# Two attentions of a fused two-block kernel: where the softmax division is done

## The reference, cut to what matters

```python
def gqa_block(q_blk, k, v):                      # first block
    s = jnp.einsum('bkgqd,bksd->bkgqs', q_blk, k).astype(jnp.float32) * (HEAD_DIM ** -0.5)
    p = jax.nn.softmax(s, axis=-1)
    return jnp.einsum('bkgqs,bksd->bkgqd', p.astype(v.dtype), v)
...
    a_out = attention_branch(q, k, v, q_g, k_g, cos, sin, n_tok) * jax.nn.silu(a_gate)
...
def block(args):                                 # second block, MLA
    s = jnp.einsum('bhqd,bhkd->bhqk', qi, kt).astype(jnp.float32) * scale
    s = jnp.where(mask[None, None], s, -1e30)
    pr = jax.nn.softmax(s, axis=-1).astype(vt.dtype)
    return jnp.einsum('bhqk,bhkd->bhqd', pr, vt)
```

## Time and profile before

| what | us |
|---|---|
| median of 3 runs | 2500.69 |
| the profiled execution, its own time | 2496.18 |
| its span (first to last instruction) | 2494.4 |
| first attention | about 360 to 626 |
| MLA | about 1146 to 1460 |
| mean granted TensorE clock | 0.919 of full speed |

### The profile page before, as it was taken

The page is one execution under the profiler, slowest core; times in us unless marked ns, Lnnn a source line. Parts: engine busy times, 40 slices in busy tenths (PEclk is TensorE's granted clock), DMA queues, the critical chain, the costliest instruction groups (busy, mean ns, idle before and its releaser), DMA issues.

```text
span 2494.4 us, 24100 instructions
## 1 busy us (share of the span) xinstructions
PE 2153.5 (86%) x9931; PEld 1760.8 (71%) x9931; DVE 1213.3 (49%) x1423; ACT 606.8 (24%) x1035; POOL 892.0 (36%) x493
## 2 busy tenths in 40 slices
PE   4998988888887889975877879599999999999868
PEld 4976756666765777754656667488888888888657
DVE  5252148888667444226566544633233333333674
ACT  3011227776112000123444431310000000000421
POOL 3322215554332333221344233244334433433443
PEclk9998999999988999977878779699999999999979
DMA  3112100000312111100000021011111111112012
GB/s 132 43 34 72 43 0 1 1 1 1 110 34 101 34 41 36 34 26 10 9 17 17 1 96 48 9 51 43 51 51 49 45 51 51 45 49 68 26 42 76
DMA packets 30268, 102.90 MB, mean 41 GB/s; under 512 B 3216, under 2 KB 5008, under 8 KB 30160
## 3 DMA queue, kind: packets, MB, share of 16 engines
q1 hardware_dynamic: 21456, 77.72, 9.9%
q10 hardware_dynamic: 8704, 23.65, 2.5%
HBM read 92.97 MB, written 8.39 MB: 41 GB/s over the span
## 4 chain that ended last, share of the span: by engine, by line
PE 72%; DVE 19%; ACT 5%; issue 3%; POOL 0%; DMA 0%; ACTq 0%; SPq 0%; DVEq 0%; POOLq 0%
PE psb L290 20%; PE psa L290 20%; PE psd L290 9%; PE psc L290 8%; DVE tiny L891 2%; PE psd L1580 2%; PE psc L1543 1%; PE psd L807 1%; DVE tiny L1511 1%; PE psc L311 1%; DVE qks L1449 1%; DVE gl L1979 1%; PE psc L785 1%; DVE ptl L907 1%; PE psd L311 1%
## 5 line engine op out<-in xcount | busy, mean ns | idle before, releaser
L301 POOL TENSOR_TENSOR wh<-wraw,one 128x1024 fp32r<-128x1024 f32 x140 | 272.5, 1946 | 1056.9 <-PE psa L290 417.7
L304 POOL TENSOR_TENSOR wl<-wraw,wh 128x1024 fp32r<-128x1024 f32 x140 | 364.3, 2602 | 11.0
L952 POOL TENSOR_TENSOR pb<-pb,tiny 128x1024 f32<-128x1024 f32 x64 | 121.2, 1894 | 184.6 <-DVE tiny L901 184.3
L290 PE MATMUL psa<-mh,wh 128*128 128x512 f32 x480 | 153.1, 401 | 36.3 <-ACT mh L966 14.0
L290 PE MATMUL psa<-ml,wh 128*128 128x512 f32 x480 | 152.9, 400 | 6.9 <-DVE ml L1764 2.4
L290 PE MATMUL psa<-mh,wl 128*128 128x512 f32 x480 | 150.5, 395 | 0.0
L290 PE MATMUL psb<-mh,wh 128*128 128x512 f32 x480 | 150.1, 394 | 0.0
L290 PE MATMUL psb<-ml,wh 128*128 128x512 f32 x480 | 148.7, 391 | 0.0
L290 PE MATMUL psb<-mh,wl 128*128 128x512 f32 x480 | 148.7, 391 | 0.0
L290 PEld LDWEIGHTS psa<-mh,wh 128*128 128x128 f32 x480 | 91.7, 193 | 57.5 <-ACT rraw L1176 14.1
L290 PEld LDWEIGHTS psa<-ml,wh 128*128 128x128 f32 x480 | 90.8, 192 | 32.4 <-DVE ml L1764 4.6
(11 more groups left out here) (519 smaller groups left out, 4960.4 us busy)
## 6 DMA issues: line engine op xcount, KB each, us to landing
wraw<-slabs SPq DMA_DIRECT2D x140, 512.0 KB, 3.5
x<-xT SPq DMA_DIRECT2D x8, 520.0 KB, 9.3
h<-xT ACTq DMA_DIRECT2D x8, 512.0 KB, 6.4
residual<-h ACTq DMA_DIRECT2D x8, 512.0 KB, 5.5
h<-residual ACTq DMA_DIRECT2D x8, 512.0 KB, 7.6
outT<-ob ACTq DMA_DIRECT2D x8, 512.0 KB, 2.6
ct<-dft ACTq DMA_DIRECT2D x1, 1300.0 KB, 5.9
st<-dft ACTq DMA_DIRECT2D x1, 1300.0 KB, 8.8
```

Source lines behind the costliest of these rows:

```text
L290: t = e.matmul(o, lhsT=lw, rhs=xx(kt, c0, cn), start=n == 0, stop=n == total - 1, skip_group_check=True)
L301: e.tensor_tensor(WH[j][:, :], RAW[:, j, :], ONE[:, 0:1].to_broadcast([P, 1024]), MUL).then_inc(*pooled.up(("high", s)))
L304: e.tensor_tensor(WL[j][:, :], RAW[:, j, :], WH[j][:, :], SUB).then_inc(*pooled.up(("split", s)))
L952: e.tensor_tensor(PB[v][:, :], PB[v][:, :], RI[:, v:v + 1].to_broadcast([P, T]), MUL)
```

## The change

The exponentials are turned and split as they are. TensorE no longer waits for GpSimd before it turns a unit, only for ScalarE. VectorE adds and inverts the sums of four units in one instruction of 128x4 once per group. A new function turns each of the four columns of reciprocals, read with a step of zero as a 128x128 tile, into PSUM (L823 of the new kernel in the first attention, L1609 in MLA), so that each query's reciprocal lies in every partition, and VectorE multiplies the group's output with it. In the first attention that multiplication stands where the gate's was, and the gate's goes to GpSimd (L972 of the new kernel). In MLA it is a second instruction behind the sum. GpSimd's list loses both attentions' multiplications, and its splits of MLA's slabs follow one another.

```diff
--- before.py
+++ after.py
@@ -708,7 +708,8 @@
 
         NU, NG = 64, 16
         LAG, AHEAD = 3, 7
-        MXM, NB, RSA, RSM, RI = (TINY[:, 4 * n:4 * n + 4] for n in range(1, 6))
+        MXM, NB = (TINY[:, 4 * n:4 * n + 4] for n in range(1, 3))
+        RSA, RSM, RI = ([TINY[:, c:c + 4] for c in (c0, c1)] for c0, c1 in ((12, 0), (16, 32), (20, 36)))
         MXT = TINY[:, 24:32]
         scale1 = HD ** -0.5
...
                 e.wait_ge(*vec.on(("meta low", g - 3)))
             elif g >= 1:
                 e.wait_ge(*acted.on(("meta s", g - 1)))
+            if g >= 4:
+                e.wait_ge(*vec.on(("out", g - 4)))
             for v in range(4):
                 c0 = (4 * (g % 2) + v) * P
...
@@ -776,7 +779,7 @@
             t.then_inc(*psum.up(("s", u)))
 
         def pe_turns(e, u):
-            e.wait_ge(*pooled.on(("p", u)))
+            e.wait_ge(*acted.on(("exps", u)))
...
@@ -786,8 +789,10 @@
                 t.then_inc(*psum.up(("turned", u, h)))
 
         def pe_meta_turn(e, g):
-            e.wait_ge(*pooled.on(("p", 4 * g + 3)))
+            e.wait_ge(*acted.on(("exps", 4 * g + 3)))
...
@@ -809,6 +814,15 @@
             if third == 2:
                 t.then_inc(*psum.up(("out", g)))
 
+        def pe_sums_spread(e, g):
+
+            e.wait_ge(*vec.on(("one over", g)))
+            e.wait_ge(*acted.on(("meta s", min(g + 3, NG - 1))))
+            e.wait_ge(*vec.on(("meta low", g)))
+            for v in range(4):
+                t = e.transpose(PS[Dp][:, 0, v * P:v * P + P], RI[g % 2][:, v:v + 1].to_broadcast([P, P]), SQC[:, 0, :])
+            t.then_inc(*psum.up(("sums spread", g)))
+
         def pe_attention(e):
             pe_values_in(e)
@@ -819,6 +833,8 @@
                 g, phase = divmod(u - AHEAD, 4)
                 if g >= 0 and phase == 1:
                     pe_meta_turn(e, g)
+                if g >= 0 and phase == 3:
+                    pe_sums_spread(e, g)
                 if 0 <= u - LAG < NU:
                     pe_turns(e, u - LAG)
...
@@ -875,7 +893,7 @@
                     mine, rest = slice(64 * s, 64 * s + 64), slice(64 - 64 * s, 128 - 64 * s)
                     e.wait_ge(*psum.on(("out", g)))
                     if g >= 2:
-                        e.wait_ge(*vec.on(("gated", g - 2)))
+                        e.wait_ge(*pooled.on(("gated", g - 2)))
                     e.activation(OT[g % 2][mine, :], PS[Dp][rest, 1, :], ACT.Copy).then_inc(*acted.up(("out low", g)))
                 if u % 4 == 1 and u < NU - 4:
...
@@ -893,12 +911,13 @@
             e.tensor_scalar(NB[:, v:v + 1], MXM[:, v:v + 1], MXT[:, 4 * (g % 2) + v:4 * (g % 2) + v + 1], -scale1,
                             MAX, MUL).then_inc(*vec.up(("bias", u)))
 
-        def dve_norms(e, u):
-            v = u % 4
-            e.wait_ge(*acted.on(("exps", u)))
-            e.tensor_tensor(RI[:, v:v + 1], RSA[:, v:v + 1], RSM[:, v:v + 1], ADD).then_inc(*vec.up(("all sum", u)))
-            e.wait_ge(*vec.on(("all sum", u)))
-            e.reciprocal(RI[:, v:v + 1], RI[:, v:v + 1]).then_inc(*vec.up(("one over", u)))
+        def dve_sums(e, g):
+            if g >= 2:
+                e.wait_ge(*psum.on(("sums spread", g - 2)))
+            e.wait_ge(*acted.on(("exps", 4 * g + 3)))
+            e.tensor_tensor(RI[g % 2], RSA[g % 2], RSM[g % 2], ADD).then_inc(*vec.up(("all sum", g)))
+            e.wait_ge(*vec.on(("all sum", g)))
+            e.reciprocal(RI[g % 2], RI[g % 2]).then_inc(*vec.up(("one over", g)))
 
         def dve_parts(e, u):
@@ -910,15 +929,15 @@
                                 ).then_inc(*vec.up(("p low", u, h)))
 
         def dve_outputs(e, g):
-            tile, s, c0 = g // 4, (g // 2) % 2, (g % 2) * HALF
+            s = (g // 2) % 2
             mine = slice(64 * s, 64 * s + 64)
+            o = OT[g % 2][mine, :]
             e.wait_ge(*acted.on(("out low", g)))
-            e.tensor_tensor(OT[g % 2][mine, :], OT[g % 2][mine, :], PS[Dp][mine, 1, :], ADD
-                            ).then_inc(*vec.up(("out", g)))
-            seg = GT[mine, tile + 4, c0:c0 + HALF]
-            e.wait_ge(*vec.on(("out", g)))
-            e.scalar_tensor_tensor(out=seg, in0=OT[g % 2][mine, :], scalar=0.5, in1=seg, op0=MUL, op1=MUL
-                                   ).then_inc(*vec.up(("gated", g)))
+            e.tensor_tensor(o, o, PS[Dp][mine, 1, :], ADD).then_inc(*vec.up(("out sum", g)))
+            e.wait_ge(*vec.on(("out sum", g)))
+            e.wait_ge(*psum.on(("sums spread", g)))
+            e.scalar_tensor_tensor(out=o, in0=o, scalar=0.5, in1=PS[Dp][mine, 0, :], op0=MUL, op1=MUL
+                                   ).then_inc(*vec.up(("out", g)))
 
         def dve_attention(e):
@@ -932,8 +951,8 @@
                     dve_stage(e, 2 * (u // 16) + 2)
                 if u < NU:
                     dve_maxima(e, u)
-                if 0 <= u - 1 < NU:
-                    dve_norms(e, u - 1)
+                if 0 <= u - 1 < NU and (u - 1) % 4 == 3:
+                    dve_sums(e, (u - 1) // 4)
                 if 0 <= u - LAG < NU:
                     dve_parts(e, u - LAG)
@@ -945,13 +964,12 @@
                     dve_meta_max(e, u // 4 + 1)
 
         def pool_attention(e):
-            e.wait_ge(*vec.on("v low"))
-            for u in range(NU):
-                v, g = u % 4, u // 4
-                e.wait_ge(*vec.on(("one over", u)))
-                e.tensor_tensor(PB[v][:, :], PB[v][:, :], RI[:, v:v + 1].to_broadcast([P, T]), MUL)
-                e.tensor_tensor(PM[g % 2][:, v, :], PM[g % 2][:, v, :], RI[:, v:v + 1].to_broadcast([P, META]), MUL
-                                ).then_inc(*pooled.up(("p", u)))
+            for g in range(NG):
+                tile, s, c0 = g // 4, (g // 2) % 2, (g % 2) * HALF
+                mine = slice(64 * s, 64 * s + 64)
+                seg = GT[mine, tile + 4, c0:c0 + HALF]
+                e.wait_ge(*vec.on(("out", g)))
+                e.tensor_tensor(seg, OT[g % 2][mine, :], seg, MUL).then_inc(*pooled.up(("gated", g)))
 
 
@@ -1020,7 +1038,7 @@
             spread(e, C, ACC1[:, :], "r1 spread")
 
         def act_out1(e):
-            e.wait_ge(*vec.on(("gated", NG - 1)))
+            e.wait_ge(*pooled.on(("gated", NG - 1)))
             for m in range(KT):
                 load(e, f"h{m}", H[:, m, :], xT[m][:, 0:T])
...
+
+        def dve_mla_sums(e, U):
+
+            r = RI[U // 4 % 2]
             e.wait_ge(*acted.on(("mexp", U)))
-            e.reciprocal(RI[:, v:v + 1], RSA[:, v:v + 1]).then_inc(*vec.up(("mone over", U)))
-
-        def pool_mla_norms(e, U):
-            v, n = U % 4, U % 8 * P + P
-            e.wait_ge(*vec.on(("mone over", U)))
-            e.tensor_tensor(LPB[U % 8][:, 0:n], LPB[U % 8][:, 0:n], RI[:, v:v + 1].to_broadcast([P, n]), MUL
-                            ).then_inc(*pooled.up(("mp", U)))
+            if U >= 8:
+                e.wait_ge(*psum.on(("msums spread", U - 8)))
+            e.reciprocal(r, RSA[U // 4 % 2]).then_inc(*vec.up(("mone over", U)))
         def pe_mla_turns(e, U):
             h, u = divmod(U, 8)
-            e.wait_ge(*pooled.on(("mp", U)))
+            e.wait_ge(*acted.on(("mexp", U)))
             if u == 3 and h + 1 < MH_ or U == 0:
                 e.wait_ge(*vec.on(("v2", h + 1 if u == 3 else 0)))
             elif U >= 1:
                 e.wait_ge(*vec.on(("lp low", U - 1)))
             for kt in range(u + 1):
+                if kt == 4 and u == 4:
+                    e.wait_ge(*vec.on(("mout", U - 1)))
                 t = e.transpose(PS[C][:, kt // 4, (kt % 4) * P:(kt % 4) * P + P], LPB[u][:, kt * P:kt * P + P],
                                 SQC[:, 0, :])
@@ -1581,6 +1601,15 @@
                                  start=kt == 0 and hl == 0, stop=kt == nk - 1 and hl == 1, skip_group_check=True)
             t.then_inc(*psum.up(("o", U)))
 
+        def pe_msums_spread(e, U):
+            if U % 8 == 3 and U // 8 + 1 < MH_:
+                e.wait_ge(*vec.on(("v2", U // 8 + 1)))
+            e.wait_ge(*vec.on(("mone over", U)))
+            for v in range(4):
+                t = e.transpose(PS[C][:, 1, v * P:v * P + P], RI[U // 4 % 2][:, v:v + 1].to_broadcast([P, P]),
+                                SQC[:, 0, :])
+            t.then_inc(*psum.up(("msums spread", U)))
+
         def act_mla_out(e, U):
             h = U // 8
@@ -1593,7 +1622,10 @@
             h, g = U // 8, U % 8 // 4
             mine = slice(64 * (h % 2), 64 * (h % 2) + 64)
             e.wait_ge(*acted.on(("mout", U)))
-            e.tensor_tensor(MX[mine, 4 + h // 2, g * HALF:g * HALF + HALF], MOT[mine, :], PS[Dp][mine, 1, :], ADD
+            e.tensor_tensor(MOT[mine, :], MOT[mine, :], PS[Dp][mine, 1, :], ADD).then_inc(*vec.up(("mout sum", U)))
+            e.wait_ge(*vec.on(("mout sum", U)))
+            e.wait_ge(*psum.on(("msums spread", U)))
+            e.tensor_tensor(MX[mine, 4 + h // 2, g * HALF:g * HALF + HALF], MOT[mine, :], PS[C][mine, 1, :], MUL
```

(18 more changed lines are left out.)

15 lines of the change are left out of this document (10 added, 5 removed).

## The result

The changed kernel took 2519.28 us (median of 4, 2517.76 to 2520.89), the kernel before 2500.43 beside it: ratio 1.0076, 95% interval 1.0063 to 1.0089. It is slower, by 18.9 us; forecast were 2521 and a range of 2501 to 2540. The profiled execution took 2518.69 with a span of 2516.8, 22.4 more than before's span.

The account below looks back on a forecast made before the run. The prediction saw a relay between TensorE, ScalarE and VectorE as the bound, not GpSimd. Terms of 6.1 + 2.2 (attention) + 12.8 (MLA) made 21.1 us, so 2517 profiled and 2521 for the median, range 2501 to 2540.

Parts of the forecast that it names:

- a relay and not GpSimd: Whole kernel: engines wait on each other in turn; GpSimd, busy 892 of 2494 us, can't be the bound by amount.
- The wait for the copy, 6.1 us: First attention: reciprocals' turn waits for ScalarE's meta-score copy, delaying 7 ordinary groups by 0.4 and 6 staging ones by 0.55.
- VectorE's wait before the sum stays near 0.7: First attention, sign of being right: VectorE's idle time before adding the output half, 0.72 us before, hardly changes.
- The end of the attention, 2.2: End of first attention: later value products +0.7, reciprocals' turn ahead of the last unit's +0.5, last gate on GpSimd +1.0.
- MLA's first groups, 0.65 each: MLA, heads' first groups: second 64x512 VectorE instruction on the path, net 0.65 us each, 5.2 us for eight.
- MLA's second groups, 0.35 each by the exclusion: MLA, second groups beside slab splits: GpSimd and two-SBUF-input VectorE instructions exclude each other; 0.35 us, 1.75 for 5 heads.
- Start of MLA, 2.0: MLA's start: the first split now falls beside VectorE instructions that ran alone, costing one wait of 2.0 us.
- Last head, 2.0 for the stall and 0.65 + 0.65 + 0.65 + 0.72 for the four products behind it, 4.7: MLA's last head: a split arrives where GpSimd had none, a 2.0 us wait; added products lengthen its groups too.
- C: Rival, first attention: TensorE, idle longer before turns, drops to 1.2 GHz, +15 us, 2536; chance 0.13.
- A: Rival: VectorE's list decides in first attention, new turns fit TensorE's idle time; 0.5 us slower, 2501; chance 0.11.
- B: Rival, faster: in MLA GpSimd's splits run clear of VectorE, ending the lock's waits; -6 us, 2495; chance 0.10.
- D: Rival, first attention: the wait for the copy is hidden, the rest as forecast; 12.4 us slower, 2513; chance 0.16.

## Why the prediction was right

- **What bounds it**, a relay and not GpSimd: right as to GpSimd. 188.5 us less of GpSimd and the time went up.
- **The wait for the copy, 6.1 us**: right as the cause, as far as the wait and the four instructions behind it are taken as one (the run that moves them gives nearly 9 back), and right in the sum, 6.6 over twelve groups. Its composition was not: 0.4 to 0.55 a group was forecast, nine have 0.2 to 0.3, and three have 1.5 through the clock, so the sum came out by luck. The step "VectorE's wait before the sum stays near 0.7" failed: it is 1.20. Its low part ends 3.3 us behind the copy in both kernels, and ScalarE's output half comes 0.5 later.
- **The end of the attention, 2.2**: 2.6 in this execution (44.6 against 42.0 us from the last copy to the next stage), but other executions of the same code had up to 47.3. The last gate takes 1.26 us on GpSimd, where 1.0 stood for it.
- **MLA's first groups, 0.65 each**: right at the full clock, 0.67 in three heads. Half of the cases with a projection behind them were missed: in the other three the group was 2.2 longer, 1.55 of it a projection at 1.2 GHz. That makes 4.7 us that the forecast's sum does not have. The six together have 8.7, where 3.9 were forecast.
- **MLA's second groups, 0.35 each by the exclusion**: the six slots up to the last head's have 2.1 in all, where 1.75 and 0.5 were forecast (from the second head's query product to the last head's it is 235.7 us against 225.0; 8.7 of the difference are the first groups). The mechanism is shown by the held splits.
- **Start of MLA, 2.0**: wrong. VectorE came first and GpSimd waited; from the first query product to the second it is 19.67 us against 19.53. GpSimd's instruction took 4.36 us there:

```profile
1167.44 1.90 POOL L301 TENSOR_TENSOR wh<-wraw,one 128x1024 fp32r<-128x1024 f32 x1 [40.18 <-PE psd L290]
1169.41 4.36 POOL L304 TENSOR_TENSOR wl<-wraw,wh 128x1024 fp32r<-128x1024 f32 x1
```

- **Last head, 2.0 for the stall and 0.65 + 0.65 + 0.65 + 0.72 for the four products behind it, 4.7**: wrong in the result. The stall is there (3.19 us at 1422.85, 1.22 before), but from the last head's query product to the next stage it is 68.57 us against 68.56. The granted clock there was 0.79 in place of 0.67. In both first groups of the stretch six turns took 1.51 us before and 0.84 now, and the next turns followed 0.46 us sooner, which covers most of the product. Of the second one, before and now:

```profile
1444.38 1.51 PE L1543 MATMUL psc<-sqc,lp 128*128 128x128 f32 x6 [3.23 <-DVE ltl L1564]
...
1447.31 1.73 PE L1543 MATMUL psc<-sqc,lp 128*128 128x128 f32 x7 [1.41 <-DVE ltl L1564]
```

```profile
1467.69 0.84 PE L1563 MATMUL psc<-sqc,lp 128*128 128x128 f32 x6 [2.00 <-DVE ltl L1584]
...
1470.15 1.73 PE L1563 MATMUL psc<-sqc,lp 128*128 128x128 f32 x7 [1.62 <-DVE ltl L1584]
```

So the forecast left out that TensorE was at 1.2 GHz here before the change. Of the fourteen traces eleven took 68.3 to 69.7, with the stall and without; the other three took 70.5, 71.8 and 72.7. The clock is part of this, but the stretch at 0.67 and the one at 0.79 were equally long; what sets its length was not tested apart.
- **The rivals.** C (the clock) was given a chance of its own with 15 us on top. It was no rival but a part: some 4 us in the attention and 4.7 in MLA, and the terms that fell away in MLA (start and last head, 6.7 us forecast, 0.2 measured) made room for it. That the time came out within 2 us is luck, by sizes that offset each other. The reading behind C was also wrong in its order: the low clock did not begin behind the idle stretch ahead of 476.06, for the score products from 474.02 on took 0.63 us already. Of the chances, 0.10 for no change and 0.11 for faster do not fit A's 0.11 and B's 0.10; they seem to be exchanged. B fell as a way to a faster kernel: with the splits held on purpose the kernel was still at 1.0061. A and D fell with the groups' length.

Open stays what makes the clock fall in every second head. In the two heads above TensorE's waits before the projection are alike (1.24 and 1.63, 1.22 and 1.51 us), and the first is at 0.39 us a product, the second at 0.63; before the change a wait of 2.86 us stood there, and its projection was at 0.39. The Trainium skill (TensorE: Matmul & The Clock Gate, A second HAM failure mode: psum-queue depth-cycling) tells of a kernel whose short pauses between groups of products make the clock swing between its two levels. The trace agrees in that TensorE changes between its two levels here too, with waits of 1.2 to 1.6 us between groups of instructions; no run here separates the cause.

## What to carry to other kernels

A new instruction can cost more by where it waits than by its length: put it in each engine's list behind the work that others wait for, and give each reader of a bank its own signal (sum and product), so that a release does not come with the later of two. Here the first gave 9 us back; the second gave nothing by itself, and kept 25 us from being lost once the product stood late. Where TensorE works in bursts, a stall of 2 us taken away can come back as a lower clock, so read the granted clock by group and head, and not its mean over the kernel, which here was 0.919 and 0.922. And when a sum comes out right, check its terms: here two terms, 6.7 us together, came to nothing, and the clock filled the gap.
